# Head norm of the attention on one root for all heads: sums in four 32-column tiles, one reciprocal, four one-row products that spread it

## The reference, cut to what matters

```python
def rmsnorm(x, g):
    xf = x.astype(F32)
    y = xf * lax.rsqrt(jnp.mean(xf * xf, axis=-1, keepdims=True) + EPS)
    return (y * g.astype(F32)).astype(x.dtype)
...
        o = attention(q, k, v, lam, l)                                  # (B, S, 4 heads, 128)
        y_b = (rmsnorm(o, subln_g[l]) * (1.0 - lam_init)).reshape(B, S, ATTN_WIDTH)
        y_c, h_re, h_im = ssm_mix(...)
        mix = jnp.concatenate([y_a, y_b, y_c], axis=-1).astype(x.dtype)
        x = x + g1 * (mix @ w_out[l])
        h2 = rmsnorm(x, norm2_g[l]) * (1.0 + sc2) + sh2
        x = x + g2 * moe_ffn(h2, ...)                                   # 64 experts, top 8, one shared
```

## Time and profile before

| | us |
|---|---|
| median of 3 runs (1965.66 to 1969.91) | 1968.53 |
| the profiled execution | 1961.67 |
| its span | 1959.6 |
| PE busy (share of the span) | 1758.8 (90%) |
| DVE busy | 681.2 (35%) |
| ACT busy | 343.9 (18%) |
| POOL busy | 693.1 (35%) |

### The profile page before, as it was taken

One profiled execution on the slowest core, in us unless ns is written; L12 is line 12 of the kernel. 1 busy time (PEld: TensorE's weight loads), 2 busy tenths in 40 slices (PEclk: granted clock), 3 DMA queues, 4 the chain that ended last, 5 costly groups with the idle time before them and its releaser, 6 DMA issues.

```text
span 1959.6 us, 28101 instructions
## 1 busy us (share of the span) xinstructions
PE 1758.8 (90%) x11199; PEld 1009.8 (52%) x11199; DVE 681.2 (35%) x1672; ACT 343.9 (18%) x761; POOL 693.1 (35%) x754
## 2 busy tenths in 40 slices
PE   6897877999999999999589788888999999999974
PEld 3672466455555555555267336644555555555533
DVE  4873345312222322211479533551221222222216
ACT  3131312111112111111021231211111111111101
POOL 1214001545454455454011130053445445454420
PEclk9987689999999999999779778988999999999996
DMA  9447644999999999999934673679999999999943
GB/s 302 150 153 246 193 183 169 399 392 324 381 409 390 375 369 381 370 360 351 345 104 131 200 264 133 247 280 415 392 368 366 375 358 377 370 358 371 371 160 138
DMA packets 216640, 588.89 MB, mean 301 GB/s; under 512 B 67706, under 2 KB 147278, under 8 KB 162623
## 3 DMA queue, kind: packets, MB, share of 16 engines
q1 hardware_dynamic: 146224, 506.99, 68.0%
q0 software_dynamic: 67232, 79.73, 11.9%
q10 hardware_dynamic: 3054, 0.38, 0.2%
HBM read 775.22 MB, written 56.95 MB: 425 GB/s over the span
## 4 chain that ended last, share of the span: by engine, by line
PE 74%; DVE 9%; DMA 8%; issue 5%; SPq 2%; ACT 2%; POOL 1%; POOLq 0%; DVEq 0%; ACTq 0%
PE ps L1328 34%; PE ps L1341 15%; PE ps L898 8%; PE ps L1053 4%; DMA xg<-hrows,idx_x 4%; PE ps L1230 2%; PE ps L941 2%; DMA ypart<-yrows_k 2%; PE ps L1280 1%; SPq L616 1%; PE ps L927 1%; DMA vbuf<-in_cache_v 1%; DMA raw<-in_w_ada 1%; DVE vbuf L1984 1%; PE ps L1257 1%
## 5 line engine op out<-in xcount | busy, mean ns | idle before, releaser
L1328 PE MATMUL ps<-raw,xTs 128*64 128x256 f32 x6144 | 746.6, 394 | 1.7 <-ACT xTs L1587 1.4
L1328 PEld LDWEIGHTS ps<-raw,xTs 128*64 128x64 f32 x6144 | 419.4, 136 | 269.8 <-issue 38.9
L847 POOL DMA_INDIRECT yrows_k<-ytok,idx_y x192 | 196.5, 1023 | 510.4 <-DVE ytok L2009 466.7
L1341 PE MATMUL ps<-dn,scratch 128*64 128x512 f32 x1536 | 361.6, 592 | 1.5 <-DVE scratch L2013 1.5
L2003 DVE TENSOR_TENSOR scratch<-scratch,ps 128x128 f32<-128x128 f32 x192 | 55.1, 287 | 716.5 <-ACT scratch L1609 716.4
L840 POOL DMA_INDIRECT xg<-hrows,idx_x x192 | 197.6, 1029 | 123.5 <-DVE idx_x L2097 65.2
L2009 DVE COPY ytok<-ps 128x512 f32<-128x512 f32 x192 | 132.7, 691 | 213.8 <-PE ps L1341 213.8
L1587 ACT ACTIVATE xTs<-ps 128x512 f32<-128x512 f32 x192 | 114.4, 597 | 422.2 <-PE ps L898 422.2
L1341 PEld LDWEIGHTS ps<-dn,scratch 128*64 128x64 f32 x1536 | 108.0, 135 | 145.3 <-issue 110.6
L898 PEld LDWEIGHTS ps<-cst,xg 128*128 128x128 f32 x768 | 81.5, 142 | 181.1 <-issue 146.1
L1609 ACT ACTIVATE scratch<-ps 128x128 f32<-128x128 f32 x192 | 53.2, 277 | 639.4 <-PE ps L1328 639.3
(11 more groups left out here) (371 smaller groups left out, 1478.6 us busy)
## 6 DMA issues: line engine op xcount, KB each, us to landing
raw<-in_exp_w_gate SPq DMA_DIRECT2D x128, 1024.0 KB
raw<-in_exp_w_up SPq DMA_DIRECT2D x128, 1024.0 KB
dn<-in_exp_w_down SPq DMA_DIRECT2D x128, 1024.0 KB, 9.2
wide<-in_w_ada SPq DMA_DIRECT2D x32, 1024.0 KB, 7.8
wide<-in_w_in SPq DMA_DIRECT2D x16, 1024.0 KB, 8.2
ypart<-yrows_k SPq DMA_DIRECT2D x16, 1024.0 KB, 11.9
raw<-in_w_ada SPq DMA_DIRECT2D x14, 1024.0 KB, 12.7
kbuf<-in_cache_k POOLq DMA_DIRECT2D x32, 256.0 KB, 3.3
```

What stands on the lines that cost most here:

```text
L847: pool.indirect_dma_start(yrows_k.rearrange("t (h d) -> (t h) d", h=2), bass.IndirectOffsetOnAxis(ap=idx_y[:, b:b + 1], axis=0), ytok[n % ...
L1328: ins = mm(ps[64 * h:64 * h + 64, 2 + n % 2, 0:256], xTs[n % 2][:, k % 4, 64 * (k // 4):64 * (k // 4) + 64], w[:, k, h], start=k == 0, sto ...
L1341: ins = mm(ps[64 * h:64 * h + 64, 5 + n % 2, :], actT[:, n % 2, 64 * j:64 * j + 64], dn[n % NDOWN][:, j, 512 * h:512 * h + 512], start=j = ...
```

## The change

Each head is squared on its own, right after its copy to `oT`. The sums use only 32 columns of the ones and a tile of PE's array for each head, so that all four heads' sums lie in one bank: head h on partitions 32h to 32h+31. Scale, root and reciprocal then run once over 128 x 264, all heads at a time. To bring each head's reciprocal roots back to all 128 partitions, four products with one row of ones (partition 32h, tile of 32 rows) write banks 4 to 7. They stand in PE's list between the first parts of c = 1 and c = 2. DVE makes one instruction for each head out of the products with `oT` and with the gain, and raises `attn_mixed` head by head; PE waits for it head by head in c = 0.

```diff
-    osd = vflat[:, HEADS * T:2 * HEADS * T].rearrange("p (h t) -> p h t", h=HEADS)
+    oroot = vflat[:, HEADS * T:HEADS * T + T]
...
-                    sp.wait_ge(attn_mixed.sem, attn_mixed.by(layer, 1))
+                    sp.wait_ge(attn_mixed.sem, attn_mixed.by(layer, HEADS))
...
-            W(o_squared)
             W(w_copied, 2 * HEADS)
             for h in range(HEADS):
-                ins = mm(ps[:, 4 + h, 0:T], ones, osq[:, h, :], start=True, stop=True)
+                W(o_squared, h + 1)
+                ins = mm(ps[32 * h:32 * h + 32, 4, 0:T], ones[:, 0:32], osq[:, h, :], start=True, stop=True,
+                         skip_group_check=True, tile_position=(0, 32 * h))
             ins.then_inc(o_sums.sem, 1)
...
                 for k in ks:
+                    if c == 0 and k in out_order[4:]:
+                        W(attn_mixed, k - 1)
                     ins = mm(ps[:, c % 4, 0:T], w[:, k, P * (c % 2):P * (c % 2) + P], mixT[:, k, :],
...
                 out_part(c, out_order[:4])
-            W(attn_mixed)
+                if c == 1:
+                    W(o_root)
+                    for h in range(HEADS):
+                        mm(ps[:, 4 + h, 0:T], ones[32 * h:32 * h + 1, :], oroot[32 * h:32 * h + 1, :], start=True, stop=True,
+                           skip_group_check=True, tile_position=(32 * h, 0)).then_inc(o_spread.sem, 1)
             for c in range(4):
                 out_part(c, out_order[4:]).then_inc(out_made.sem, 1)
...
                     act_(oT[:, h, 0:NP_], ps[:, 4, 0:NP_], ACT.Copy).then_inc(pv_copied.sem, 1)
+                    if h == 0:
+                        W(o_ready)
+                    W(pv_copied, h + 1)
+                    act_(osq[:, h, :], oT[:, h, :], ACT.Square).then_inc(o_squared.sem, 1)
             ada_columns(WIDE_ADA - 1, 4, 256)
-            W(o_ready)
-            W(pv_copied, HEADS)
-            act_(osq, oT[:, :, :], ACT.Square).then_inc(o_squared.sem, 1)
             W(o_var)
-            act_(osd, osd, ACT.Sqrt).then_inc(o_sd.sem, 1)
-            W(o_normed)
-            act_(mixT[:, 2:6, :], osd, ACT.Copy, scale=sm[:, 7:8]).then_inc(attn_mixed.sem, 1)
+            act_(oroot, oroot, ACT.Sqrt).then_inc(o_sd.sem, 1)
...
             W(o_sums)
-            ts(osd, ps[:, 4:4 + HEADS, 0:T], 1.0 / VD, EPS, ALU.mult, ALU.add).then_inc(o_var.sem, 1)
+            ts(oroot, ps[:, 4, 0:T], 1.0 / VD, EPS, ALU.mult, ALU.add).then_inc(o_var.sem, 1)
             W(o_sd)
+            v.reciprocal(oroot, oroot).then_inc(o_root.sem, 1)
             W(o_ready)
             W(pv_copied, HEADS)
-            chain(v.reciprocal(osd, osd))
-            tt(osd, osd, oT[:, :, :], ALU.mult).then_inc(o_normed.sem, 1)
+            for h in range(HEADS):
+                W(o_spread, h + 1)
+                stt(mixT[:, 2 + h, :], ps[:, 4 + h, 0:T], sm[:, 7:8], oT[:, h, :], ALU.mult, ALU.mult)\
+                    .then_inc(attn_mixed.sem, 1)
```

More of the change, by code:

```diff
@@ L431, in program @@
     pv_copied = sig("pv_copied", HEADS)
-    o_squared, o_sd = sig("o_scalar", 2).parts()
+    o_squared = sig("o_squared", HEADS)
+    o_sd = sig("o_sd", 1)
     o_sums = sig("o_sums", 1)
@@ L435, in program @@
     chosen_ready, sh_act, rows_ready, spare_ready, gk_ready, gsel_ready = sig("route_vector", 6).parts()
-    o_var, o_normed = sig("o_vector", 2).parts()
-    attn_mixed = sig("attn_mixed", 1)
+    o_var, o_root = sig("o_vector", 2).parts()
+    o_spread = sig("o_spread", HEADS)
+    attn_mixed = sig("attn_mixed", HEADS)
     pool_prompt = sig("pool_prompt", 1)
```

## The result

The changed kernel takes 1957.3 us in the median of 12 runs (1952.8 to 1962.5), the kernel before 1969.2 beside it (12 runs, 1962.5 to 1975.5). The ratio is 0.9937 [0.9924, 0.9949]: 12.4 us faster, by the interval 10 to 15. The forecast was 1953.6, within 1949 to 1961.

A forecast was written before the change was run, and what follows sets the result against it. PE was taken as the bound (74% of what ended last), standing still during the head norm's chain. Gains of 7.4 and 7.5 us in the two layers, together 14.9, gave 1968.5 - 14.9 = 1953.6 us, range 1949 to 1961.

The forecast's parts named there:

- Squares: Head norm, ACT: the 1.07 us square leaves the path; four small squares hide under ACT's waits and cost nothing.
- The fear that a square pushes the attention loop: Attention loop, ACT: a square standing before L1540 delays it; without cover, 1.8 us a layer.
- Sums: Head norm, PE: eight matmuls on four overlapping 32-column tiles take 1.1 us at half clock instead of 3.87.
- tiles don't overlap: Rival, sums and spread: the small matmuls run one by one, gain 9.8 us in all, 1958.7; chance 0.14.
- Root, wait, spread: Head norm: root ready at 243.4, PE there at 246.3, so no wait; spread takes 0.65 us.
- The bound of 1.8 us without overlap: Spread on PE: upper bound for its eight matmuls, 8 x 0.223 us, if the tiles don't overlap.
- Clock at the head norm: PE reaches full clock 5.4 us after the sums begin; 2.15 us lost a layer.
- The local sum: Head norm: gains of 7.4 us in the first layer and 7.5 in the second, together 14.9.
- What comes behind: After the fourth finished block, all releases move along with the engines, so the whole 14.9 us counts as gained.
- The experts' start: Rival, expert loops: waits at their start grow 7.1 us in one layer (1960.7, chance 0.09) or eat everything (0.05).

The follow-up runs named there:

- spread_first: Changed kernel with the four one-row spread products moved ahead of the first part of c = 0; ratio 0.9962 to the kernel before.
- the filled kernels: Unread products keep PE busy where it stood idle, added to the changed kernel (0.9901), to it without tiles (0.9906) and to the kernel before (0.9991).
- no_tiles_again: Second run of the changed kernel with sums and spread on the whole array instead of tiles; 0.9918, 1951.7 us.
- after: The changed kernel itself, first measurement against the kernel before; 0.9937, 1957.3 us.
- after_again: The changed kernel, unaltered, run once more against the kernel before; 0.9935, 1954.4 us.
- one_square: Changed kernel with one square of all four heads again, behind the last modulation copy; ratio 0.9926 to the kernel before.
- both root_later: Changed kernel with one or three further unused reciprocals of 264 columns ahead of the true one; 0.9955 and 0.9956.
- both no_tiles: Two runs of the changed kernel with sums and spread on the whole array instead of tiles; 0.9913 and 0.9918.
- root_later_5: Changed kernel with three further unused reciprocals ahead of the true one, root 5.4 us later; ratio 0.9956 to the kernel before.

## Why the prediction was right

*Squares.* Right that ACT's 1.07 us go and that head 3 is hidden: the sums start 0.04 us behind ACT's copy. The fear that a square pushes the attention loop did not come true: behind each of the first three heads' squares ACT stands idle for 1.4 to 2.0 us before it goes on.

*Sums.* Tiles overlap, as said. Sized at 1.1 us, took 0.66: I counted the half clock, and they ran at full, which PE had kept from the attention loop. Half clock gives 1.11 (spread_first). The rival "tiles don't overlap" (1958.7) is out, though its time is nearer to the measured one than the forecast: the same sum came about another way.

*Root, wait, spread.* Right: scale 0.43, reciprocal 1.80, root at 244.4, PE there at 246.9, no wait, spread 0.66 for 0.65. The bound of 1.8 us without overlap is what the whole array takes (1.94). One row on each of four row tiles costs what the sums' four column tiles of all rows do (0.66). The Trainium skill, TensorEngine Tiling (Array Packing), Key Properties, says that a change of the tiling mode drains the engine. The trace can't show a drain as such; it leaves at most some 0.2 us for both changes around the spread (0.66 in the chain, two turns of 0.22), so the rule costs next to nothing here.

*Clock at the head norm.* Counted 5.4 us from the sums' start to full clock; it was 4.1 (240.87 to about 245.0), with the first 0.7 or so of it, the sums, at full clock. The local sum was too small by that and by the sums: 16.3 us won, not 14.9. To the second part of c = 0 it is 10.4 us from the copy, where I had 11.0. Another 1.9 us in both layers lie ahead of the copy, from the clock of the modulation products; no step of the change makes them.

*What comes behind: the step that failed.* "I count the whole 14.9 as gained." The releases do move along, but the same work behind them doesn't take the same time. Counted from the last value product, both layers together have won 18.2 us at the norm's sums, 15.9 at the shared expert and 13.5 at the fourth expert step. So 4.7 of 18.2 are given back, where I had nothing. They lie in four places:

- the router took 5.61 and 5.64 us and takes 6.75 and 6.73 (2.2 in both layers);
- the last 16 table products took 2.02 in either layer and take 2.61 and 2.65 (1.2);
- the 32 matmuls of the first expert step took 5.70 and 5.67 and take 5.97 and 5.87 (0.5);
- the second step follows them 0.4 and 0.3 us later than it did (0.7).

The first three are time at half clock. The last is not: ACT takes up the first step's result 0.75 us behind the end of the matmuls in the first layer (0.11 before), and what holds it the profile doesn't show. For the router the filled kernels bear it out: where it takes 3.77 us in every kernel, nothing is lost up to the shared expert. Why the same stretch gets more half clock in one kernel than in another, no run shows. The first step came at 335.9, not 333.5, of which 1.4 is the later start of the head norm in this execution. By the last expert step 9.9 us are left in this profile and 12.9 in the second one of the same kernel, around the timed 12.4.

*The experts' start.* I gave 0.14 to a loop that takes 7.1 us or more. The first loop grew by 4.0, the second by 0.9, in the other profile by 1.3 and none. That is within what this start scatters by, not a step of 7 us.

*The total.* 12.4 against 14.9, inside the range. The local term was 1.4 too small (3.3 with the clock ahead of it), and the term behind it, which I had at nothing, is 4.7. The two errors partly cancel, and that they do is luck: the number looks better than its working.

## What to carry to other kernels

Before you price work on a path, ask how many columns each step needs: a root of a per-token sum needs one row a head, and here that turned a chain through PE, DVE and ACT that PE waited for into a list of PE with 2.5 us to spare. Then walk behind the gain: wherever PE stands idle and restarts, a shift upstream can be shortened or swallowed (2.1 us became nothing here), so measure a local gain behind the next restarts too, not only where it is made. And repeat a profile before you split a few microseconds of total time by it.

## What the runs showed of the hardware that I had not expected

- Restarts can swallow upstream differences. The same 16 router matmuls took 5.28 (no_tiles_again) to 6.75 us (after) in kernels that differ only some 40 us ahead, and 3.77 with PE kept busy. In seven profiles (after, after_again, one_square, both root_later, both no_tiles) the arrivals at the fourth expert step lie together, 116.7 to 118.3 us in the first layer and 117.1 to 118.1 in the second (root_later_5 with 121.1 aside), while the norm's sums of the same profiles differ by up to 3.1 us. Larger shifts come through in part: spread_first is 5.3 and 5.5 us behind at the norm's sums and 3.1 and 3.4 at the fourth step.
- Products without use can pay: filling the idle stretches gave 6.8 us in the changed kernel, and nothing clear in the one before. They can also hurt: a filling that ran at half clock at first took 8.44 us for 5.61 and stood in the way of real work.
- Eight products on four 32-column tiles take 0.66 us at full clock and 1.11 at half, on one row the same 0.66 at full; on the whole array the sums took 3.60 at half and the spread 1.94 at full.
- The clock at the head norm is partly inherited: the same eight modulation products, with nothing changed in or ahead of them, took 1.06 us in one layer and 1.88 in another of one kernel (after_again).
- Two kernels that differ locally by 2 us a layer in one direction differ in time, twice, in the other: by 4.7 us by the ratios of different comparisons (0.9913 and 0.9937), by 2.7 side by side (1951.7 and 1954.4). With intervals of about 2.5 to 4 us to either side that may be chance; what else it could be is open.
